# Twelve expert rows a phase move from the first attention stage to the gate stage in VectorE's row plan

## The reference, cut to what matters

```python
for l in range(DEPTH):                              # 2 layers
    mix = token_mixers(h, ...)                      # A: band attention, B: RG-LRU, C: differential attention,
    h = layer_norm(DEEPNORM_ALPHA * h + mix, ...)   # G: sigmoid gates * branch projections, O: output projection
    ff = peer_ffn(h, ...)
    h = layer_norm(DEEPNORM_ALPHA * h + ff, ...)

def peer_ffn(...):   # per token: 8 heads, top 16 of 16384 experts each
    ...
    hid = jax.nn.gelu(jnp.einsum('td,thkd->thk', xb, u[experts]))
    return jnp.einsum('thk,thkd->td', g * hid, v[experts])
```

## Time and profile before

| | us |
|---|---|
| median of 3 runs | 3535.96 (3531.65 to 3537.88) |
| profiled execution, its own time | 3533.43 |
| span in its trace, first to last instruction | 3531.3 |
| busy: PE / VectorE / ScalarE / GpSimd | 2925.1 / 2493.0 / 843.0 / 1844.8 |
| DMA | 1295.97 MB, mean 367 GB/s |

### The profile page before, as it was taken

How to read it: one execution, slowest core, us unless ns; L and a number is a source line. 1 busy time by engine, 2 the same in 40 slices (tenths; PEclk the granted TensorE clock), 3 DMA queues, 4 the chain that set the end, 5 groups by cost and what they waited for, 6 DMA issues and landing times.

```text
span 3531.3 us, 33020 instructions
## 1 busy us (share of the span) xinstructions
PE 2925.1 (83%) x10296; PEld 1862.3 (53%) x10296; DVE 2493.0 (71%) x5300; ACT 843.0 (24%) x2407; POOL 1844.8 (52%) x1508
## 2 busy tenths in 40 slices
PE   8999688798799878787689878888789878877777
PEld 6677444366587534355477534356478444422222
DVE  1421567787887886888888876788797887754545
ACT  2320122222210122322210123322220123332223
POOL 0000144686677534577676634587577634554554
PEclk9999899999899989998799989999799999999999
DMA  4334499999999999999999999999999999999997
GB/s 163 111 108 154 152 419 420 414 368 395 335 392 409 408 401 417 421 407 409 364 398 409 409 387 409 421 382 394 360 361 409 409 417 418 416 421 422 421 421 331
DMA packets 281580, 1295.97 MB, mean 367 GB/s; under 512 B 31808, under 2 KB 32064, under 8 KB 211776
## 3 DMA queue, kind: packets, MB, share of 16 engines
q0 software_dynamic: 216576, 1073.84, 75.7%
q1 hardware_dynamic: 64544, 218.99, 16.5%
q10 hardware_dynamic: 288, 1.05, 0.1%
HBM read 1291.65 MB, written 2.10 MB: 366 GB/s over the span
## 4 chain that ended last, share of the span: by engine, by line
PE 47%; DMA 24%; DVE 13%; POOL 7%; issue 6%; ACT 3%; DVEq 0%; SPq 0%; POOLq 0%; ACTq 0%
PE bank L594 20%; DMA ring<-in_peer,eidx 18%; PE bank L847 11%; DMA work<-in_peer,eidx 6%; POOL ring L1192 5%; PE bank L798 5%; DVE ring L1225 3%; PE bank L809 3%; DVE acc L1230 2%; PE bank L669 2%; PE bank L645 1%; POOL ring L1187 1%; ACT dg L943 1%; PE bank L624 1%; PE bank L648 1%
## 5 line engine op out<-in xcount | busy, mean ns | idle before, releaser
L1225 DVE CUSTOM_DVE_ANT_0 ring<-ring,hp 128x1024 f32<-128x1024 f32 x816 | 984.0, 1221 | 303.3 <-DMA ring<-in_peer,eidx 302.4
L1192 POOL DMA_INDIRECT ring<-in_peer,eidx x808 | 986.8, 1221 | 398.0 <-issue 221.8
L847 PE MATMUL bank<-ring,dg 128*128 128x512 f32 x1784 | 837.0, 617 | 261.7 <-ACT dg L943 231.2
L1187 POOL DMA_INDIRECT ring<-in_peer,eidx x390 | 480.5, 1232 | 920.2 <-DVE eidx L1331 423.8
L594 PE MATMUL bank<-xt,panel 128*128 128x256 f32 x4096 | 922.8, 383 | 19.8 <-ACT xt L949 5.7
L594 PEld LDWEIGHTS bank<-xt,panel 128*128 128x128 f32 x4096 | 783.6, 192 | 152.7 <-issue 30.8
L847 PEld LDWEIGHTS bank<-ring,dg 128*128 128x128 f32 x1784 | 336.5, 196 | 734.9 <-issue 697.7
L1230 DVE SCALAR_TENSOR_TENSOR acc<-ring,wgt,acc 128x1024 f32<-128x1024 f32 x326 | 415.7, 1286 | 24.8 <-DMA ring<-in_peer,eidx 21.9
L847 PE MATMUL bank<-work,dg 128*128 128x512 f32 x704 | 328.7, 610 | 106.7 <-ACT dg L943 100.5
L1225 DVE CUSTOM_DVE_ANT_0 work<-work,hp 128x1024 f32<-128x1024 f32 x208 | 252.6, 1222 | 121.6 <-DMA work<-in_peer,eidx 121.4
L1187 POOL DMA_INDIRECT work<-in_peer,eidx x154 | 195.5, 1269 | 232.9 <-PE bank L847 151.9
(11 more groups left out here) (180 smaller groups left out, 2467.8 us busy)
## 6 DMA issues: line engine op xcount, KB each, us to landing
panel<-in_panels SPq DMA_DIRECT2D x368, 512.0 KB, 6.8
ring<-in_peer,eidx POOLq DMA_INDIRECT x1198, 17.0
work<-in_rel_bias SPq DMA_DIRECT2D x16, 512.0 KB, 8.0
work<-in_peer,eidx POOLq DMA_INDIRECT x306, 22.0
gb<-in_ln_g SPq DMA_DIRECT2D x8, 512.0 KB, 8.4
gb<-in_ln_b SPq DMA_DIRECT2D x8, 512.0 KB, 10.5
panel<-in_keys SPq DMA_DIRECT2D x16, 256.0 KB, 6.4
work<-in_x SPq DMA_DIRECT2D x4, 512.0 KB, 4.6
```

The lines of the kernel that those rows point to most:

```text
L847: ins = mm(pa[t * 2 + half][:, :], dg[:, i % DIAGS, :], v_row[:, half * 512:(half + 1) * 512], start=(n == group[0]), stop=(n == group[-1]))
L1187: pool.indirect_dma_start(slots(slot, 2), None, t_in["peer"], bass.IndirectOffsetOnAxis(ap=eidx[:, 0, t, c:c + 1], axis=0)).then_inc(row_i ...
L1192: pool.indirect_dma_start(slots(slot, 1), None, one_row, bass.IndirectOffsetOnAxis(ap=eidx[:, which, t, c:c + 1], axis=0)).then_inc(row_in ...
L1225: v.tensor_tensor_reduce(row, row, hp[:, t, :], 1.0, 0.0, ALU.mult, ALU.add, hid[:, t, c:c + 1]).then_inc(used, 1)
```

## The change

Only the table differs. Stage A has 48 rows between its units' parts instead of 60, and stage G has 76 after its steps instead of 64, in phases 1 to 3.

```diff
-MIXER_ROWS = {"A": (16, 60), "B": (10, 22), "C": (12, 40), "R": 6, "G": (10, 64), "O": 16, "N": 4, "T": 16}
+MIXER_ROWS = {"A": (16, 48), "B": (10, 22), "C": (12, 40), "R": 6, "G": (10, 76), "O": 16, "N": 4, "T": 16}
```

## The result

| | before | after |
|---|---|---|
| median on the same chip, us | 3532.48 (3523.6 to 3537.88, 6 runs) | 3552.88 (3545.77 to 3561.64, 6 runs) |
| profiled execution, its own time | 3533.43 | 3545.77 |
| span in its trace | 3531.3 | 3544.0 |

The ratio is 1.0055, its interval 1.0036 to 1.0073: 12.7 to 25.8 us slower, where +15 was the sum and 3550 us the forecast.

What follows compares the result with a forecast made beforehand. DMA was taken to set the pace from G's backlog to the end of T. Phases of +10.5, -0.6 and +7.4 us, less 2 swallowed, gave +15, forecast 3550 us; range +8 to +25 (3544 to 3561).

Steps and rivals of the forecast that it cites:

- What bounds the kernel: From G's backlog to the end of T and into the next phase, DMA sets the pace, though PE looks full in G.
- VectorE in A: Fewer rows ahead of the diagonals shorten PE's waits in A: 3.9, 16 and 7.0 us gained in phases 1 to 3.
- Clock: In A, a shorter PE pause leaves a higher clock: 1.0 us gained in phases 1 and 3 each, bounds 0 and 2.4.
- DMA's 15.4 us a phase: Twelve gathers a phase lie undone at the start of G and cost their transfer, 1.28 us each, from there on.
- In exchange for idle DMA in A: The gathers undone at G's start are paid for by idle DMA in A, whose rate falls to some 350 GB/s.
- G's stretch stays near 135 us: G of phase 1 keeps its length at 406 to 409 GB/s, with VectorE waiting for landings in the last steps.
- rival C: Late merges in G delay the choice of experts, DMA runs dry, delay counts twice: up to 9.3 us more a phase, chance 0.12.
- Swallowed: Later gathers cost less where VectorE or PE is late anyway in O, L and T: 2 us in all, bounds 0 to 10.6.
- The sum: Whole kernel: phases +10.5, -0.6 and +7.4 us, together +17.3, less 2, is +15 us.
- A (faster): PE sets G's length, so rows there are free and only the gains stand: 29 us less, 3507 us, chance 0.13.
- B (swallowed by T): T's idle DMA time takes up most of the delay: about the same time, 3539 to 3543 us, chance 0.20.

Runs made afterwards that it cites:

- x2: Changed kernel with every U and V gather fetching 2 KB a partition instead of 4: 3444.05 us, ratio 0.9744 to the kernel before.
- x1: Kernel before with every U and V gather fetching 2 KB a partition instead of 4: 3475.13 us, ratio 0.9835 to the kernel before.
- x5: Changed kernel with two rows after each step of G gathered at half their bytes: 3518.4 us, ratio 0.9933 to the kernel before.
- x6: Kernel before with twelve rows a phase moved from G to A (A 72, G 52) in phases 1 to 3: 3539.71 us, ratio 1.0009.
- x8: Kernel before with fifteen rows leaving G in phases 1 and 3 for VectorE's gaps in A (4 and 5) and B (6): 3532.91 us, ratio 0.9987.
- x9: Kernel before with phase 2 changed; in phases 1 and 3 eight rows leave G, six for B, two for C: 3517.07 us, ratio 0.9963.

## Why the prediction was right, and where its steps were off

**What bounds the kernel: right.** That G runs at DMA's limit although PE looks full (132.89 of 134.9 us) was the choice on which the sign hung. x2 against x1 shows the other sign as soon as bytes are cheap (31 us faster), and x5 shows that the bytes of twelve gathers a phase are worth more than the whole loss. But a full DMA queue did not yet make G longer before the change: with half the bytes G of phase 1 kept its length (132.0 and 131.9 us). DMA and PE stood at their limits in it together, and that is why twelve gathers more cost their whole transfer.

**VectorE in A: right.** Stage A became 6.9, 15.6 and 8.0 us shorter, where 3.9 + 1.0, 16 and 7.0 + 1.0 stood. Between the starts of `weigh` of unit 0 and of unit 3, the clock's gain not counted, it is 5.1, 18.1 and 8.2 us for 3.9, 16 and 7.0. The waits fell to 3.68 and 3.69 us where about 4 was said. In phase 2 the 30.2 us of waits are 9.4, somewhat more than the "few us or less" that were named.

**Clock: right in size.** After a pause of 3.68 us the products took 4.99 us instead of 6.04, a gain of 1.05 where 1.0 was taken, at a granted clock of 0.67 instead of 0.54. In phase 3 it was 6.27 and 4.99. But a pause of 3.50 us had left them at 3.63, so the length of the pause alone does not give the price, and 1.0 was a guess between the bounds that came out well.

**DMA's 15.4 us a phase: right in kind, a little small.** G to L grew by 16.6, 16.1 and 17.1 us.

**"In exchange for idle DMA in A": wrong in the place.** The forecast had A's rate fall to 350. It stayed (374 and 379, share 0.98 and 0.99). What DMA lacks in A of phase 1 lies in its first 60 us, where GpSimd's issue sets the pace and slots do not, so there was little idle time to trade there. A to C together gained 8.8, 18.0 and 10.2 us, 37.0 where the sum had 28.9. 30.5 of them are in A itself. The other 6.5 are in B and C, which the sum put at nothing. 3.8 of these are C of phase 2, and they don't follow the rows: it took 90.3 to 90.7 us in three of the ten profiles, that of x6 among them, and 94.3 to 94.9 in the others, with the change or without. The idle time came up in B: 72.2 us at 358 instead of 394 GB/s are 2.6 MB, 6.4 us. 8.8 and 6.4 together are 15.2 of the 15.4 us that were removed ahead of G in phase 1. That split is arithmetic on one pair of profiles, not an experiment.

**"G's stretch stays near 135 us": wrong.** It is 148.4, because the forecast let the landings hold VectorE in the last steps without asking what the late merges do to PE. The waits come to 21.1 us, 16.8 of them in the second half of the stage, and PE then waits 12.13 us. That is the first half of rival C. Its second half, that DMA runs dry behind it and the delay counts twice, did not come: O to L still run at 408 GB/s with a share of 1.03, as before (409, 1.03). The loss appears once, 14.0 us in G and 2.6 in O to L, where the forecast had it behind G.

**Swallowed: right.** T gained 0.6, 0.7 and 1.1 us, 2.4 together where 2 was taken. Differences of this size lie within the spread of single executions.

**The sum.** +49.8 (G to L) - 37.0 (A to C) - 2.4 (T) is +10.4 for the profiled executions; their phases differ by 10.7, and the spans by 12.7. The runs say +20, 12.7 to 25.8. +15 lay between the two. By the profiles the mis-sized terms are the gains ahead of G (8 us too small) and the backlog (3.6 too small), which partly cancel, and that they do is luck.

**Rivals.** A (faster) fell with G's 405 GB/s; x2 is the kernel in which it is true (31 us faster against the 29 that A counted). B (swallowed by T) fell with T's 2.4 us.

## What to carry to other kernels

Before moving work between stages, ask of each stage whether its DMA queue has room, and not only which engine is idle: a stage whose gathers land 20 us later than in an empty queue has none, even if the engine that uses them waits for something else. Moving the use of data moves its transfer. If a move leaves DMA idle ahead of a saturated stage, the loss comes back there, whatever hid in the source stage.

Rows belong just ahead of a place where DMA idles because the engine that starts the gathers waits for free slots (here C: share 0.91, GpSimd waiting 18.7 us). They gain nothing ahead of a place where DMA idles because that engine is itself at its limit (here the first 60 us of A: share 0.93, one gather in 1.8 us), nor in a mere gap of the engine that uses them. A stage's mean share and rate can hide this (A: 374 GB/s at 0.98), so cut the stage into parts before you read them.

## What the runs showed of the hardware that I had not expected

- GpSimd needs 0.94 us to start a gather of 128 rows at some times and up to 1.99 at others, with 0.30 us before each. In the first 60 us of stage A of phase 1 this comes to 1.8 us a gather before the change, longer than the 1.28 us of its transfer. In this part DMA falls to 338 to 364 GB/s at a share of 0.93 to 0.97 in before, after, x6, x8 and x9, whatever number of rows stands there. Behind it the share is 1.01 to 1.03. What makes an issue long was not tried.
- Two queues are behind by different times: in G of the kernel after gathers land 28.3 us after their issue, panels 6.8 us.
- Phase 0, whose program is the same in all kernels, ended between 694.9 and 706.3 us in ten profiles, so a difference of 10 us between the whole spans of two single executions says nothing here. In the stretch from 150 to 210 us PE's granted clock was 1.00 in the kernel before and 0.89 in x6, and PE got through 215 matmuls there in 53.08 us where it had got through 234 in 51.49. What makes the clock differ there is open.
